# Banded attention scores with a split-precision q: second pass over 64 rows, an even and an odd head side by side

## What is computed

```python
    qb = q.reshape(B, nb, BLOCK, A_KV_HEADS, A_REP, HEAD_DIM)      # 8 blocks of 128, 2 groups, 4 heads, 64
    ...
    kb = jnp.concatenate([kp[:, :-2], kp[:, 1:-1], kp[:, 2:]], axis=2)   # a block and its two neighbours
    ...
    scores = jnp.einsum('bnqgrd,bnkgd->bngrqk', qb, kb).astype(jnp.float32)
    scores = scores * (HEAD_DIM ** -0.5)
    ...
    scores = jnp.where(mask[None, :, None, None], scores + bias[None, None], -jnp.inf)
    ...
    p = jnp.exp(scores - m)
    denom = jnp.sum(p, axis=-1, keepdims=True) + jnp.exp(sink_l - m)
    out = jnp.einsum('bngrqk,bnkgd->bnqgrd', probs, vb)
```

## Time and profile before

| | |
|---|---|
| median of 3 runs | 622.42 us (622.28 to 623.08) |
| profiled execution, its own time | 622.04 us |
| its span | 620.2 us |
| busy: PE, DVE, ACT, POOL | 611.6, 440.1, 357.9, 317.9 us |
| products on PE, each with a weight load | 3252 |
| L1746 and L1747, the two score passes | 64 and 64 products, 20.1 and 20.3 us |

### The profile page before, as it was taken

The page is one execution under the profiler, slowest core; times in us unless marked ns, Lnnn a source line. Parts: engine busy times, 40 slices in busy tenths (PEclk is TensorE's granted clock), DMA queues, the critical chain, the costliest instruction groups (busy, mean ns, idle before and its releaser), DMA issues.

```text
span 620.2 us, 9411 instructions
## 1 busy us (share of the span) xinstructions
PE 611.6 (99%) x3252; PEld 501.6 (81%) x3252; DVE 440.1 (71%) x854; ACT 357.9 (58%) x769; POOL 317.9 (51%) x303
## 2 busy tenths in 40 slices
PE   8999999999999999999999999999999999999996
PEld 7889888888888888888887777777777777888885
DVE  5773326333444429998999798989988898789684
ACT  6652223223334227877786777788787778633563
POOL 4634004403656532536547777887787789510701
PEclk9999999999999999999999999999999999999999
DMA  7630016365685720101015833224323423499043
GB/s 258 202 131 1 0 57 233 127 255 183 224 268 212 247 68 1 34 2 35 1 27 131 217 74 87 63 59 99 81 61 77 103 86 137 141 334 372 1 150 122
DMA packets 49934, 76.90 MB, mean 124 GB/s; under 512 B 5656, under 2 KB 25632, under 8 KB 49760
## 3 DMA queue, kind: packets, MB, share of 16 engines
q1 hardware_dynamic: 49728, 76.04, 39.4%
q10 hardware_dynamic: 160, 0.27, 0.1%
HBM read 46.54 MB, written 20.05 MB: 107 GB/s over the span
## 4 chain that ended last, share of the span: by engine, by line
PE 94%; DVE 3%; ACT 2%; DMA 1%; issue 0%; POOL 0%; DVEq 0%; ACTq 0%
PE ps L1565 18%; PE ps L1567 17%; PE ps L1566 17%; PE ps L1858 10%; PE ps L1876 5%; PE ps L1875 5%; PE ps L1790 5%; PE ps L1795 5%; PE ps L1760 3%; PE ps L1810 2%; PE ps L1770 2%; PE ps L1771 1%; PE ps L1747 1%; PE ps L1746 1%; PE ps L1577 1%; DVE p_w L1301 1%
## 5 line engine op out<-in xcount | busy, mean ns | idle before, releaser
L1419 DVE TENSOR_TENSOR pT_lo<-ps,pT_hi 128x512 fp32r<-128x512 f32 x128 | 88.2, 691 | 16.5 <-ACT pT_hi L1032 16.5
L1032 ACT ACTIVATE pT_hi<-ps 128x512 fp32r<-128x512 f32 x128 | 76.0, 596 | 36.7 <-PE ps L1858 36.4
L744 POOL TENSOR_SCALAR p_b<-p_b,stat 128x1024 f32<-128x1024 f32 x64 | 71.9, 1123 | 36.5 <-DVE stat L1414 36.4
L1565 PE MATMUL ps<-hT_hi,w_hi 128*128 128x512 f32 x208 | 84.1, 404 | 0.0
L1567 PE MATMUL ps<-hT_hi,w_lo 128*128 128x512 f32 x208 | 81.5, 392 | 0.0
L1566 PE MATMUL ps<-hT_lo,w_hi 128*128 128x512 f32 x208 | 81.2, 390 | 0.0
L1858 PE MATMUL ps<-ident,p_b 128*128 128x128 f32 x512 | 78.1, 276 | 0.2
L1409 DVE TENSOR_REDUCE stat<-ps 128x1 f32<-128x1024 f32 x64 | 77.7, 1215 | 0.7 <-PE ps L1810 0.6
L1858 PEld LDWEIGHTS ps<-ident,p_b 128*128 128x128 f32 x512 | 60.9, 140 | 21.0 <-issue 7.6
L1021 ACT ACTIVATE p_b<-ps,stat 128x1024 f32<-128x1024 f32 x64 | 71.3, 1114 | 6.7 <-DVE stat L1409 5.1
L1875 PE MATMUL ps<-pT_hi,vB 128*128 128x512 f32 x128 | 55.4, 433 | 0.0
(11 more groups left out here) (217 smaller groups left out, 1478.7 us busy)
## 6 DMA issues: line engine op xcount, KB each, us to landing
w_raw<-w_in SPq DMA_DIRECT2D x13, 512.0 KB, 4.6
x_in<-x SPq DMA_DIRECT2D x8, 512.0 KB, 3.4
wt_raw<-w_out SPq DMA_DIRECT2D x8, 512.0 KB, 4.5
t_scratch<-wt_hi SPq DMA_DIRECT2D x16, 256.0 KB, 2.6
t_scratch<-wt_lo SPq DMA_DIRECT2D x16, 256.0 KB, 2.6
q<-q_h SPq DMA_DIRECT2D x16, 256.0 KB, 3.6
wn_raw<-w_in SPq DMA_DIRECT2D x8, 336.0 KB, 3.7
k<-k SPq DMA_DIRECT2D x9, 256.0 KB, 2.9
```

The lines of the kernel that those rows point to most:

```text
L744: nc.gpsimd.tensor_scalar(p_b[:, (U + 1) % 4, :], p_b[:, (U + 1) % 4, :], r_b[:, U % 4:U % 4 + 1], 0.5, ALU.mult, ALU.mult).then_inc(s_bp, 1)
L1032: nc.scalar.activation(pT_hi[:, 1 - G % 2, 4 * a:4 * a + 4, U % 4 * P:(U % 4 + 1) * P], ps[:, 4 + a, :].rearrange("p (k c) -> p k c", c=P) ...
L1419: nc.vector.tensor_tensor(pT_lo[at_], ps[:, 4 + a, :].rearrange("p (k c) -> p k c", c=P), f(pT_hi[at_]), ALU.subtract).then_inc(s_bTl, 1)
L1565: nc.tensor.matmul(o, a_hi, b_hi, start=first, stop=False, skip_group_check=goes_on)
```

## The change

The high part of q of an odd head goes to rows 64 to 127 of `q_st` and its low part to rows 0 to 63; even heads stay. The first pass, over 128 rows with `k_hi2` alike in both halves, gives the same sum. The second pass multiplies by the high part of q alone, over the 64 rows where that is, so an even head uses rows 0 to 63 of the array and an odd one rows 64 to 127. The term q_lo k_lo is left out. All four first passes of a unit come ahead of its four second passes.

```diff
@@ evac_g of ACT
                         h = 2 * (m - 1) + q
-                        last = nc.scalar.activation(q_st[0:HD, h, cols], ps[HD * q:HD * (q + 1), bank, :],
+                        rows = slice(HD * q, HD * (q + 1))
+                        last = nc.scalar.activation(q_st[rows, h, cols], ps[rows, bank, :],
                                                     ACT.Copy, scale=-A_SCALE / SLOPE[h])
@@ evac_g of DVE
                         h = 2 * (m - 1) + q
+                        rows = slice(HD * q, HD * (q + 1))
                         last = nc.vector.scalar_tensor_tensor(
-                            out=q_st[HD:P, h, cols], in0=ps[HD * q:HD * (q + 1), bank, :],
-                            scalar=-A_SCALE / SLOPE[h], in1=f(q_st[0:HD, h, cols]), op0=ALU.mult,
+                            out=q_st[HD * (1 - q):HD * (2 - q), h, cols], in0=ps[rows, bank, :],
+                            scalar=-A_SCALE / SLOPE[h], in1=f(q_st[rows, h, cols]), op0=ALU.mult,
                             op1=ALU.subtract)
@@ scores_w of PE
                     q = q_st[:, REP * g + r, n * P:(n + 1) * P]
                     nc.tensor.matmul(ps[:, r, 0:w], q, k_hi2[:, g, k0:k0 + w], start=True, stop=False)
-                    nc.tensor.matmul(ps[:, r, 0:w], q, k_lo2[:, g, k0:k0 + w], start=False,
-                                     stop=True).then_inc(s_ws, 1)
+                for r in range(REP):
+                    rows = slice(HD * (r % 2), HD * (r % 2 + 1))
+                    nc.tensor.matmul(ps[:, r, 0:w], q_st[rows, REP * g + r, n * P:(n + 1) * P],
+                                     k_lo2[rows, g, k0:k0 + w], start=False, stop=True).then_inc(s_ws, 1)
```

## The result

The changed kernel takes 631.46 us (median of 4 runs, 630.91 to 631.71) against 622.37 us: a ratio of 1.0139, 95% interval 1.0127 to 1.0151. It is slower by 9.1 us. The profiled execution has a span of 629.5 us where the kernel before had 620.2.

A forecast was written before the change was run, and what follows sets the result against it. A loop between PE and DVE was taken to bound the window units. Even steps 3.60, odd 3.75, step 3 0.15, step 14 0.42, step 15 0.57, ends 0.2: 8.7 us on 622.04, 630.7, median 631.0 (626.6 to 632.8).

The forecast's parts named there:

- one loop: Window units: head 0's scores, DVE's row up to `pT_w_lo`, `pv_w`, rest of PE's step, next scores; step pair 14.08 us.
- narrow group: The 64-row second passes of a unit, in two pairs, starting 0.81 us after its scores at 384 columns, 0.58 at 256.
- turns: PE's work behind a unit's score passes, to start 1.48 us after the scores instead of 1.41 at 384 columns.
- PE's account: PE's own time over the 16 window units, pairing gain against two switches per unit: +1.6 us.
- D: Delay of a unit's first `max_w` after its scores begin: 0.75 us at 384 columns, 0.57 at 256.
- cushion: Delay that `pv_w` can take free of charge: 0.15 us in even steps, none in odd steps.
- step 14: Window step at 256 columns, to lose 0.57 - 0.15 = 0.42 us.
- Step 3: Window step whose first `max_w` is already late, so no new wait, only 0.15 us of lateness from step 2.
- The other sign: PE's waits at `pv_w` for `pT_wl` in steps 4 to 13 go from 3.0 us to about 10 us.
- PE alone decides: Whole kernel: switches free and the loop has room for D, so 5.3 us gained, 617; chance 0.06.
- the delay is hidden: Whole kernel: only PE's account with switches counts, +1.6 us at most, 623 to 624; chance 0.06.
- Half of the delay is absorbed: Even window steps give their share back, 4.5 us remain, 627; chance 0.09.
- Switches dearer: D grows by 0.10 to 0.20 us in 13 steps, 1.3 to 2.6 us, 632.4 to 633.6; chance 0.07.

The follow-up runs named there:

- order_only: Kernel before with only the order changed, four first passes then four second passes, all products over 128 rows: 628.67 us, ratio 1.0100.
- two reordered kernels: Changed kernel and kernel before, each with DVE's `o_w_sum` ahead of its first `max_w` and ACT's first `pT_w_hi` ahead of its first `exp_w`: 624.91 and 624.83 us.
- narrow_one_side: Changed kernel with all four 64-row second passes over rows 0 to 63, none beside another, `q_st` laid out as before: 631.72 us, ratio 1.0150.
- narrow_head_by_head: Changed kernel with each head's 64-row second pass directly behind its 128-row first pass, eight switches per unit, no pairs: 645.27 us, ratio 1.0360.

## Why the prediction was right

*What bounds the stage.* Right: PE and DVE in one loop, although PE reads as full. order_only shows it with nothing else changed.

*What the change saves and what it switches.* Right in sum, with one term of a different shape. The narrow group was put at 0.81 us after the scores and came at 0.80 (0.58 and 0.56 at 256 columns). The second pair starts 0.28 us behind the first: 0.18 of streaming and 0.10 of the first pair's own load, which the prediction had inside its 0.39. The turns were given as 1.48 and came at 1.35: the load exposed behind the switch lengthens the first turn rather than delaying its start, and I had put it ahead. PE's account was +1.6 us in the prediction (12 x 0.07 + 4 x 0.18). By the first gated product it is -0.01 us per unit at 384 columns and 0.09 at 256, some 0.2 us in all. The two reordered kernels, which end level, agree.

*What the order delays.* D was 0.75 and 0.57; measured 1.39 - 0.67 = 0.72 and 1.08 - 0.55 = 0.53. The runs divide it: about 0.5 from the order (order_only, 6.2 us), the other 0.2 from the switch and its load (2.8 us more to 631.46; narrow_one_side, with the old layout of `q_st`, pays the same).

*Who waits behind it, and the cushion.* Steps 4 to 13 were to grow by 5 x 0.60 + 5 x 0.75 = 6.75 us. They went from 70.2 us (scores of step 4 at 251.43, of step 14 at 321.65) to 76.9 us (252.62 and 329.54): 6.7. Even steps grew by 0.58 to 0.69 and odd ones by 0.70 to 0.72. That the total is so close is in part luck. Odd steps paid 3.54 us instead of 3.75, even ones 3.16 instead of 3.00, and the two nearly cancel. With D at 0.72 and 0.63 us paid per even step, the cushion was about 0.1 us and not 0.15: `pT_w_lo` is done at 286.80 + 0.69 = 287.49, `pv_w` starts at 287.63, and its second product follows after 0.31 us instead of 0.24, so 0.21 us goes where the prediction put 0.16. In step 14 there is no cushion at all (0.57 instead of 0.42); why is not shown. Step 3 grew by 0.09 instead of 0.15. The pair of steps 7 and 8 lasts 290.90 - 275.53 = 15.37 us, as forecast (15.4). The other sign came out only in part: the waits at `pv_w` for `pT_w_lo` were to reach about 10 us, and the view of waits has 3.5 + 4.1 = 7.6. A record of PE outlasts the distance to the next start, so the idle time behind it is shorter than the stall: the last gated product of step 8 starts at 286.84 and `pv_w` 0.79 us later, where the usual distance is 0.23, a stall of 0.56 us of which the view shows 0.41.

*The rest of the sum.* The span grew by 9.3 us against 8.7. Of the difference 0.3 stands ahead of the window units, in a stretch that the change doesn't touch (the first product of 512 columns already starts at 8.78 us into the span instead of 8.49), and some 0.2 at the end of the window stage.

*The rivals.* "PE alone decides" and "the delay is hidden" are out. "Half of the delay is absorbed" is out in the changed kernel, but it is near what the reorder on DVE and ACT does (6.5 of 9.1 us come back). "Switches dearer" is out for D. The price of a switch, 0.19 us, was in the prediction only as pieces that I didn't add up for one direction. The expectation of narrow_head_by_head had 0.27 us in, 0.27 us out and the exposed load of 0.1 us once; each switch pays that load, so a head costs 0.74 us and not 0.64. The unit came at 2.86 us to the turns where 2.2 to 2.5 was expected, 0.4 to 0.7 us in each of 16 units, and that is most of the 10 us by which the time was missed.

## What to carry to other kernels

When passes are put together by kind (all first ones, then all second ones), the last pass of the first result moves back; ask who waits for that result before counting what the engine saves. A saving on an engine that reads 99% busy is worth only what the loop through its neighbours lets through: here 10.4 us of its work left out gave 2.7. To count a loop, take all the work between the instruction that waits for the other engine and the one that the other engine waits for; moving work inside that stretch changes nothing, and moving an instruction past it needs a look at everyone who waits for that instruction.

## What the runs showed of the hardware that I had not expected

Weight loads for 128-row products hide behind the product in flight: starts lie 0.18 us apart at 384 columns. The same holds for narrow products in the same 64 rows once the first is under way (narrow_one_side: 285.68, 285.85, 286.02). Behind a switch the load is not hidden. The first narrow product of narrow_one_side starts at 285.39, its load with it, and the next start is 0.29 us away. In the changed kernel the second pair follows the first after 0.28 us; the pair itself starts as one, with both loads:

```profile
284.48 0.34 PE L1751 MATMUL ps<-k_lo,q_st 64*128 64x384 f32 x2
```

Hence two 64-row pairs take 0.55 us from the first start to the next full product. With 0.1 us of delay ahead of them, nearly nothing is left of the gain over the four 128-row products, which take 0.71. For each direction of a switch 0.19 us was measured. The rows around the 32-row group give about the same when their pieces are added, 0.10 + 0.10 us going in and 0.10 to 0.13 + 0.10 coming out.
